# Tile 1's last-mixer projection by token, with the norms of its heads as row sums, and the bias tables asked for behind the last gather

## The reference, cut to what matters

```python
def rms_norm_2(x, g):
    xf = x.astype(jnp.float32)
    y = xf * lax.rsqrt(jnp.mean(xf * xf, axis=-1, keepdims=True) + EPS)
    return (y * g.astype(jnp.float32)).astype(x.dtype)
...
        h = rms_norm_2(x, g_mix[l])
        qa, ka, va, qd, kd, vd, qm = jnp.split(h @ w_in[l], IN_SPLITS, axis=-1)

        qa = rms_norm_2(qa.reshape(b, s, NA_HEADS, hd), qk_gain[l, 0, 0])
        ka = rms_norm_2(ka.reshape(b, s, NA_HEADS, hd), qk_gain[l, 0, 1])
        va = va.reshape(b, s, NA_HEADS, hd)
        out_na = neighborhood_attention(qa, ka, va, na_rpb[l])
...
        km = rms_norm_2(km.reshape(b, -1, MEM_HEADS, hd), qk_gain[l, 2, 1])
...
        x = x + jnp.concatenate([out_na, out_dil, out_mem], axis=-1) @ w_out[l]
        x = x + hierarchical_moe(rms_norm_2(x, g_ffn[l]), w_r1[l], b_r1[l], w_r2[l], b_r2[l], w1[l], w3[l], w2[l])
```

## Time and profile before

| what | us |
|---|---|
| time, median of 3 runs (lowest to highest) | 2332.52 (2332.44 to 2333.57) |
| the profiled execution: its own time | 2327.64 |
| the profiled execution: span from first to last instruction | 2325.8 |
| last mixer's first weight slot asked for | 1714.3 |
| last gather lands | 1721.8 |
| tile 0's value projection begins (it uses that slot) | 1726.0 |
| tile 1's projection begins | 1736.2 |
| last small table asked for | 1741.5 |
| attention's transposes begin | 1805.4 |
| output projection begins | 1842.95 |
| first expert's products begin | 1890.5 |

### The profile page before, as it was taken

One profiled execution on the slowest core, in us unless ns is written; L12 is line 12 of the kernel. 1 busy time (PEld: TensorE's weight loads), 2 busy tenths in 40 slices (PEclk: granted clock), 3 DMA queues, 4 the chain that ended last, 5 costly groups with the idle time before them and its releaser, 6 DMA issues.

```text
span 2325.8 us, 30746 instructions
## 1 busy us (share of the span) xinstructions
PE 1794.3 (77%) x11142; PEld 844.1 (36%) x11142; DVE 1295.9 (56%) x3199; ACT 851.8 (37%) x2292; POOL 654.7 (28%) x604
## 2 busy tenths in 40 slices
PE   6999876696787777687778666878779997676666
PEld 3654521161352343153336112343327553222222
DVE  4868887678657767856776867456443321111111
ACT  1234454444446544444644435444333510000000
POOL 1002444434334433433343444433330300000000
PEclk9999987696797887599889657888979998878888
DMA  9998899999999999999999999999998389999998
GB/s 395 388 363 321 324 414 421 421 420 419 403 421 421 418 420 421 421 401 421 400 402 420 420 420 420 421 421 421 420 387 286 154 353 428 428 428 428 429 429 371
DMA packets 110861, 925.71 MB, mean 398 GB/s; under 512 B 12774, under 2 KB 14340, under 8 KB 17732
## 3 DMA queue, kind: packets, MB, share of 16 engines
q0 software_dynamic: 76800, 549.70, 57.5%
q1 hardware_dynamic: 33924, 374.26, 39.0%
HBM read 922.81 MB, written 6.06 MB: 399 GB/s over the span
## 4 chain that ended last, share of the span: by engine, by line
DMA 49%; PE 29%; DVE 12%; ACT 7%; issue 3%; POOL 1%; SPq 0%; DVEq 0%; POOLq 0%
DMA arena<-in_peer_uv_dram,arena 26%; DMA arena<-in_moe_pieces_dram 14%; PE summed L1481 7%; DVE y_g L2982 5%; DMA mod<-in_w_parts_dram 4%; DMA arena<-in_w_slots_dram 3%; PE gp L1557 3%; PE gp L1866 2%; DMA arena<-in_w_parts_dram 2%; PE gp L1060 2%; PE gp L1065 2%; DVE h L2772 1%; PE gp L1553 1%; ACT arena L2215 1%; PE gp L1686 1%
## 5 line engine op out<-in xcount | busy, mean ns | idle before, releaser
L1481 PE MATMUL summed<-arena 64*64 64x512 f32 x4096 | 702.0, 782 | 323.8 <-ACT arena L2215 300.3
L2982 DVE CUSTOM_DVE_ANT_0 y_g<-arena,h 128x1024 f32<-128x1024 f32 x512 | 626.9, 1224 | 404.9 <-DMA arena<-in_peer_uv_dram,arena 345.9
L1000 POOL DMA_INDIRECT arena<-in_peer_uv_dram,arena x512 | 590.9, 1154 | 898.5 <-PE summed L1481 819.2
L1481 PEld LDWEIGHTS summed<-arena 64*64 64x64 f32 x4096 | 135.6, 157 | 753.9 <-ACT arena L2215 658.5
L2209 ACT ACTIVATE arena<-arena 128x1 f32<-128x1 f32 x512 | 102.7, 201 | 576.0 <-DVE arena L2982 573.6
L1866 PE MATMUL gp<-arena,mod 128*32 128x512 f32 x1008 | 157.6, 762 | 104.2 <-DMA arena<-in_moe_pieces_dram 104.2
L2215 ACT ACTIVATE arena<-cst,arena 128x128 f32<-128x128 f32 x512 | 205.5, 401 | 16.7
L3364 DVE TENSOR_TENSOR mod<-mod,gp 128x512 f32<-128x512 f32 x8 | 5.5, 686 | 358.8 <-ACT mod L2508 358.8
L2212 ACT ACTIVATE arena<-arena 128x1 f32<-128x1 f32 x512 | 150.8, 294 | 16.6
L1866 PEld LDWEIGHTS gp<-arena,mod 128*32 128x32 f32 x1008 | 31.8, 125 | 223.3 <-DMA arena<-in_moe_pieces_dram 163.6
L2508 ACT ACTIVATE mod<-gp 128x512 f32<-128x512 f32 x8 | 4.8, 597 | 254.0 <-PE gp L1866 254.0
(11 more groups left out here) (485 smaller groups left out, 2249.1 us busy)
## 6 DMA issues: line engine op xcount, KB each, us to landing
arena<-in_moe_pieces_dram SPq DMA_DIRECT2D x93, 2048.0 KB, 25.5
arena<-in_w_slots_dram SPq DMA_DIRECT2D x43, 2048.0 KB, 12.8
arena<-in_w_parts_dram SPq DMA_DIRECT2D x48, 1024.0 KB, 9.2
mod<-in_w_parts_dram SPq DMA_DIRECT2D x27, 1024.0 KB, 9.7
arena<-in_peer_uv_dram,arena POOLq DMA_INDIRECT x512, 15.6
t_rep<-t_rows POOLq DMA_DIRECT2D x1, 3066.0 KB, 17.5
arena<-t_rep POOLq DMA_DIRECT2D x1, 2304.0 KB, 14.3
y_g<-in_moe_pieces_dram SPq DMA_DIRECT2D x1, 2048.0 KB, 21.0
```

The source lines that it names most:

```text
L1000: pool.indirect_dma_start(rowbuf[b], None, a["peer_uv"].rearrange("l n d -> (l n) d"), bass.IndirectOffsetOnAxis(ap=idx[:, col(n):col(n) + ...
L1481: mm = pe.matmul(op[o:o + HALF, b, :], diag[i:i + HALF, n % DIAGS, i:i + HALF], rowbuf[n % ROWS][i:i + HALF, D + b * 512:D + (b + 1) * 512 ...
L2982: v.tensor_tensor_reduce(y[:, t, :], rowbuf[n % ROWS][:, 0:D], h[:, t, :], 1.0, 0.0, ALU.mult, ALU.add, dots[:, c:c + 1]).then_inc(udot, 1)
```

## The change

1. The weights turn in all four places: 0, 3, 1, 2 over and over. The value slot is used for tile 1 right after the turn of the tokens, as the first group of tile 1, and its place is then free.
2. Every slot of tile 1 is one group of eight products in which the tokens are stationary and 512 columns of the weights move ("heads"). Queries and keys thus come out with the token along the partitions.
3. The norms: ACT squares the 512 columns from the accumulator (`heads_square`), DVE sums each 64 along the row (`heads_sum`), ACT takes the root of eight numbers per token (`heads_root`), DVE takes the reciprocal and multiplies while it copies the group out (`heads_scale`). PE transposes the four chunks (`turn_heads`), ACT copies them to where the scores read them, with the gain (`heads_moved`). The sums and spreads by PE for tile 1 are gone.
4. The second half of the memory's keys is now normed as a thirteenth pair of "tile0", during the last gathers.
5. POOL asks for the sixteen `na_bias` transfers directly behind the last gather (`d_h`, which was reached long before), and for `dil_bias` when the residual is there, as before. `mask_tables` stands behind the third group's `heads_scale` on DVE and still waits for all seventeen.
6. ACT does the first two heads' exponentials behind the last root and the other six behind the copy of the last group. Some semaphores of the first layer's gates are merged; the order there is the same.

```diff
-        slots.append(("in2", view(*w, c0), [("tile1", 0, 4, z)]))
-    slots.append(("in2", view(*w, 3584), [("tile1", S, 2, 20), ("rows1", 0, 1024)]))
+        slots.append(("in2", view(*w, c0), [("heads", 1)]))
+    slots.append(("in2", view(*w, 3584), [("heads", 1)]))
...
-        turns_of = dict(ada=(2, 0, 3, 1), vec=(2, 3), lead=(0, 1), last=(0, 3, 1, 2, 3, 1, 2, 3, 1, 2))
+        turns_of = dict(ada=(2, 0, 3, 1), vec=(2, 3), lead=(0, 1), last=(0, 3, 1, 2))
...
-        SPREAD_ROWS = (70, 71, 72, 73, 90, 91, 92, 93, 108, 109, 110, 111)
+        SPREAD_ROWS = (70, 71, 72, 73, 90, 91, 92, 93, 108, 109, 110, 111, 112)
...
-            pool.wait_ge(x_ready, 4 * T + 1)
-
-            pool.dma_start(dil_bias, bass.AP(tensor=t5_rep.tensor, offset=127,
-                                             ap=[[12 * TW - 1, P], [TW, 12], [1, 384]])).then_inc(bias_in, 16)
+            pool.wait_ge(d_h, 2 * T)
             W = NA_HEADS * NDR * RW
             for hh in range(NA_HEADS):
...
+            pool.wait_ge(x_ready, 4 * T + 1)
+
+            pool.dma_start(dil_bias, bass.AP(tensor=t5_rep.tensor, offset=127,
+                                             ap=[[12 * TW - 1, P], [TW, 12], [1, 384]])).then_inc(bias_in, 16)
             load_gain(5, a["g_ffn_2"][0])
...
+            def turn_heads(m):
+
+                n = turned[0]
+                pe.wait_ge(gemm_moved, head_group(m) + 1)
+                pe.wait_ge(turn_moved, n - 1)
+                for c in range(head_width(m) // P):
+                    mm = pe.transpose(tp[:, n % 2, c * P:(c + 1) * P], head_rows[m % 2][:, c * P:(c + 1) * P], ident)
+                mm.then_inc(turn_done, 1)
+                turned[0] += 1
...
+                project("in2", slice(0, 1), tile=1)
+                for m in range(6):
                     project("in2", slice(m + 1, m + 2))
+                    if m:
+                        turn_heads(m - 1)
+                    if m >= 3:
+                        last_scores(m - 3)
+                project("in2", slice(7, 8))
+                turn_heads(5)
                 last_scores(3)
...
+            def heads_square(m):
+
+                bank = gp[:, head_group(m) % 2, :]
+                act.wait_ge(gemm_done, head_group(m) + 1)
+                if m == 5:
+                    act.activation(zn[:, 1, 1024:1024 + S], bank[:, 0:S], ACT.Copy)
+                if m >= 2:
+                    act.wait_ge(t_sum, m - 1)
+                act.activation(head_square_buf[m % 2][:, 0:head_width(m)], bank[:, CH - head_width(m):CH], ACT.Square).then_inc(t_sq, 1)
...
+                move("in2", slice(0, 1), tile=1)
                 for m in range(6):
...
+                    heads_square(m)
+                    if m:
+                        heads_moved(m - 1)
+                    heads_root(m)
                 last_exp(0)
                 last_exp(1)
...
+                act.wait_ge(gemm_moved, head_group(5) + 1)
+                move("in2", slice(7, 8))
+                heads_moved(5)
+                for u in range(2, 8):
                     last_exp(u)
...
+            def heads_sum(m):
+
+                v.wait_ge(t_sq, m + 1)
+                sq = head_square_buf[m % 2][:, 0:head_width(m)].rearrange("p (h n) -> p h n", n=64)
+                v.tensor_reduce(head_sum_col[m % 2][:, 0:head_width(m) // 64], sq, AX.X, ALU.add).then_inc(t_sum, 1)
+
+            def heads_scale(m):
+
+                g, w = head_group(m), head_width(m)
+                inv = head_root_col[m % 2][:, 0:w // 64]
+                v.wait_ge(t_root, m + 1)
+                link(v.reciprocal(inv, inv))
+                v.wait_ge(gemm_moved, g)
...
-                head_inverse("block2", 0)
-                head_scale("block2", 0)
-                head_scale("block2", 1)
-                head_inverse("block2", 1)
+                for m in range(3):
+                    heads_sum(m)
+                    heads_scale(m)
                 mask_tables()
...
+                for m in range(3, 6):
+                    heads_sum(m)
+                    heads_scale(m)
+                    last_bias(m - 3)
                 last_inverse(0, 1)
...
+                last_bias(3)
                 last_inverse(2, 3)
```

204 lines of the change are left out of this document (73 added, 131 removed).

## The result

The changed kernel takes **2342.3 us** (median of 8 runs, 2333.3 to 2355.2), the kernel before 2332.5 (8 runs, 2327.2 to 2333.6). The ratio is 1.0052, 95% interval 1.0033 to 1.0070: slower by 12 us, 8 to 16 (the two medians are 9.9 apart; the ratio is the estimate that I go by). That lies in the range (2329.5 to 2346) and 6.3 us above the forecast of 2336.0. It is slower by more than 0.2%, which had a chance of 0.40; "within 0.2%" had 0.55.

What follows compares the result with a forecast made beforehand. Mostly transfers bound the kernel, with PE binding the last mixer's projection, whose gain or loss moves the end one for one. -1.5 us (PE less ACT) plus 5.0 (table stall) made +3.5 on 2332.5: 2336.0 us, range 2329.5 to 2346.

Steps and rivals of the forecast that it cites:

- The stall by the large table: Last mixer's projection: tables land at 1780, needed at 1775, so PE's seventh group waits, costing 5.0 us.
- the part that ACT takes back: Before the attention's third transpose: PE waits some 4 us for ACT's copies, so 1.5 of 5.6 us stay.
- rival 2: Last DMA engine very late with the tables, landing from 1781.5 on: stall of 11 us plus clock, 2343.5 us; chance 0.26.
- PE's work: Tile 1's projection up to the attention: 63.5 us instead of 69.2, so PE is free 5.6 us earlier.
- The copies and the thirteenth pair: Norm work between projection groups, some 3 us under 6.96, is hidden; the extra pair during the gathers costs nothing.
- The large table: Last of the bias tables: all land at 1780, with bounds at 1772 and 1788; the mask waits for them.
- One packet for one: While SP's weights are under way, POOL's table queue gets one packet for each of SP's, 18.9 per us each.
- the sign against it (over 30): If q0 shows more than 30 packets per us between 1716 and 1743, the one-for-one rule is wrong.
- the free stretch of the queue: Ten us without SP transfers, when 912 of q0's 1440 packets went before; claimed gone in the changed kernel.
- when the changed projection needs the mask: Seventh group needs the fifth's accumulator, which DVE empties behind the mask: tables are needed at 1775.
- the sum: Whole kernel: -1.5 us from PE and ACT plus 5.0 of stall gives +3.5 us, 2336.0 us.
- Rival 3: First value slot lands 2 to 3 us later, sharing with the tables; everything moves, 2333 to 2339 us; chance 0.06.

Runs made afterwards that it cites:

- wait_apart: Changed kernel with a separate semaphore for the large table, so the mask waits for the sixteen small tables alone; 2336.9 us, ratio 1.0015 to the kernel before.
- exp_ahead: wait_apart with ACT's exponentials of heads 2, 3 and 4 ahead of the last group's copies; 2329.4 us, ratio to before 0.9985; repeated, 2329.5 us, 1.0003.
- exp_alone: Changed kernel with only ACT's exponentials of heads 2, 3 and 4 moved ahead of the last group's copies; 2338.3 us, ratio to before 1.0033.
- changed, second: Changed kernel run again with nothing edited, for a second trace; 2342.6 us against 2332.4 before, ratio 1.0045.
- changed, third: Changed kernel run again with nothing edited, for a third trace; one run, 2352.7 us.
- tables_as_before: Changed kernel with POOL's old order, large table first and then the sixteen small ones; 2339.3 us, ratio to before 1.0041.
- ask_later: exp_ahead with POOL waiting for the last gather's landing before asking for the small tables; 2331.6 us, ratio to before 0.9990.
- all_together: ask_later with ACT's copy of the first pair's transposes ahead of the exponentials of heads 5 to 7; 2328.2 us, ratio to before 0.9993.

## Why the prediction was right or wrong

**In short.** The stall by the large table and the part that ACT takes back came as forecast. What the forecast lacked is the cost of TensorE's clock behind each gap (4.2 us) and 3.2 us outside the stretch. That the time still lies in the range is in part luck: the range reached up to 2346 for a landing at 1788, and no landing was that late. The nearest number is rival 2's 2343.5, and that too is luck: its stall of 11 us did not come (4.55, 1.14 and 8.11 in the three traces), and its condition, a landing from 1781.5 on, 45.3 behind the start, was met by the third trace alone (46.2).

**PE's work: right, a little too cautious.** 63.5 us were forecast up to the attention; wait_apart and exp_ahead, without a stall, take 62.4. So PE is 6.8 us earlier, not 5.6.

**ACT takes most of it: right.** The wait for ACT's copies was forecast as some 4 us and is 4.18 or 4.19 in the five traces with ACT's order of the change. In wait_apart the third transpose stands 68.8 us behind the start (69.9 forecast), 2.6 earlier than before instead of 1.5. That ACT's order is the cause is shown by exp_alone and exp_ahead.

**The copies and the thirteenth pair: nothing, right.** With no wait on the mask (wait_apart), groups follow each other at once. From the first gather's issue to the last but one's dot it is 1472 to 1475 us in all traces, with the thirteenth pair (ten) and without (three).

**The large table: the size right, a part of its cause not.** The landing was forecast 43.8 us behind the start (1780); four traces show 42.7, 39.3, 46.2 and 43.7, mean 43.0. The stall was to be 5.0; it was 4.55, 1.14, 8.11 and 5.56, mean 4.8. One packet for one holds: from 1730 to 1750 the changed kernel's second trace has 392 and 390 packets, so q0 got 19.5 per us, and the sign against it (over 30) did not come.

```profile
q1 hardware_dynamic: 392, 5.64, 86.6%
q0 software_dynamic: 390, 0.99, 14.6%
```

But I put the late landing down to the new order, which gives up the free stretch of the queue, and with the old order in the changed projection the landing was 41.0 and the loss the same, 7.1 us in the stretch; with the new order in the projection of before it was 35.1 and the loss there nothing. Why the landing spreads from 35 to 46 us with the same order is open. What turns such a landing into a stall is when the changed projection needs the mask. The forecast was 38.8 us behind the start; landing less stall is 38.1 or 38.2 in all five traces (42.7 less 4.55, 39.3 less 1.14, 46.2 less 8.11, 43.7 less 5.56, 41.0 less 2.90). There are two accumulators for eight equal groups, and DVE, which empties them, stands in the mask. Before, the mask began at 40.7 and PE lost nothing. The mask further back in DVE's list was not tried.

**What the sum left out** is what each gap does to TensorE's clock, and three small things. I had the clock only in rival 2, for a stall of 11 us, and priced it at 1.6. For the five traces with a stall:

| | gain of PE and ACT | stall | slow work behind the stall | slow work behind ACT's gap | sum | stretch less 106.7 |
|---|---|---|---|---|---|---|
| changed | -2.6 | 4.6 | 3.1 | 2.5 | 7.6 | 7.7 |
| changed, second | -2.6 | 1.1 | 0.6 | 1.6 | 0.7 | 1.2 |
| changed, third | -2.6 | 8.1 | 2.6 | 2.3 | 10.4 | 10.5 |
| exp_alone | -5.4 | 5.6 | 2.4 | 0 | 2.6 | 2.8 |
| tables_as_before | -2.6 | 2.9 | 3.6 | 2.8 | 6.7 | 7.1 |

(Slow work is what the rows take over the same work at the upper level: in the first trace behind the stall, transposes 1.11 less 0.60, scores 2.39 less 1.14, group 8.45 less 7.13; behind ACT's gap, transposes, scores and products with the values less 1.09, 1.14 and 1.09. The -2.6 is that of the third transpose in wait_apart, before the slow work; exp_alone has the 2.75 of the shorter gap too.) The step that came out short is **the sum**, -1.5 + 5.0, which has no term for the clock. Its two terms were -2.6 and 4.6 in the mean of the changed kernel's three traces, 2.0 together, and the clock adds 4.2, so the stretch is +6.5 (6.2 by the terms). What it needed was in the rows: the earlier trace rows has 8.53 for a group that takes 6.96 at the upper level, and the earlier trace rows a granted clock of 0.57 in the 25 us ahead of it.

**Rival 3 was right in kind.** The rest, 9.7 - 6.5 = 3.2, is outside the stretch. 1.3 of it: with the small tables asked for directly behind the last gather, that gather's dot comes 5.9 to 7.4 us behind the one ahead of it (eight traces) instead of 4.9 to 5.0 (five traces, ask_later, all_together and tables_as_before among them, where they are asked for later). With the part up to the projection it is 20.1 to 22.0 instead of 19.3 to 20.1. I had looked at the value slot, and the last gather itself was late. 0.4 more lies between that dot and the projection, 1.4 behind the stretch: there a product of the routing (L1083 before, L1078 after) takes 4.78 in both traces of before and 5.82 to 6.12 in the changed kernel's three. Of what decides that, these runs show nothing; tables_as_before has 4.79 too, the other changed kernels 5.12 to 5.93.

**Left open.** The first gather is issued at 243.9, 253.7 and 247.6 us in the three traces of before's projection and at 246.6 to 261.4 in the other ten, with the same instructions up to there; the means are 248.4 and 250.7. Work at the lower level behind the wait for a weight slot at 161 to 174 us is in six of the ten and in none of the three. Whether the changed kernels have the worse luck in it by nature isn't settled by so few. No run has the projection by token with everything else of before, so its own worth is known only from the trace: PE is free for the attention 6.8 us earlier.

## What to carry to other kernels

A wait of PE costs its own length and then the slow work behind it: 1.6 to 3.6 us here behind waits of 2.9 us and more, and 10.7 us in one case ahead of the first gather, behind a wait of 3.14. So a change that turns steady work into the same work with two gaps can lose, although in the mean each gap alone (4.6 and 4.2) is smaller than what was won (6.8). Put waits of an in-order engine by the first use of the data, not by the first use of its neighbour: one semaphore for all seventeen tables held up products that needed none of them. And where executions differ by 10 us and more ahead of the stage that is changed, compare stretches between two events, not ends.

## What the runs showed of the hardware

- **TensorE's level after a gap.** Behind each of nine gaps of 2.90 to 8.11 us in this stage came work at 1.2 GHz, behind four of 1.43 and 1.44 none; behind one of 1.14 half a batch of scores. The cost was 1.6 to 3.6 us each, and not in order of the gap: 3.6 behind 2.90, 2.6 behind 8.11. The length of the gap alone doesn't decide. Ahead of the same product at 161 to 174 us, gaps of 2.19 to 3.14 were followed by the lower level in six traces, and gaps of 2.61 to 2.91 were not in four. In five of the six the fall cost 1.3 to 1.7 us, in the changed kernel's first trace 10.7. A page of the Trainium skill says the same in kind: TensorE: Matmul & The Clock Gate, Part 1, has the clock fall to half when the engine has been idle and rise again when it has been busy. The traces agree with that for the nine gaps; by it the forecast should have asked of each gap what the clock would add.
- **A start that varies.** The same first instructions brought the first gather to 243.9 or 253.7 us in one kernel. In the second, three rows of sixteen products, 1.85 us each at the upper level, took 3.64, 3.57 and 3.48 at the start, where the first has 3.41, 1.85 and 1.85: the upper level was reached later. The two first gathers are 9.7 us apart by it and by what else differs up to there.
- **A gather's tail.** Asking for sixteen small transfers on the queue of a gather that is still under way made its last rows 1 to 2.4 us late (dots 5.9 to 7.4 us apart in eight traces instead of 4.9 to 5.0 in five). The Trainium skill, DMA: Bandwidth & Descriptors, section "Queues, rings and completion order", says that each DMA engine takes the descriptors of a queue in their order, but that a later one may finish its write before an earlier one. That leaves room for it; no run here shows the mechanism.
